# The up projection's steps of 512 columns, two sums on the way out of PSUM, and the first block's convolution moved behind the rest

## The reference

```
h = rms_norm(x, ffn_norm)
u = causal_depthwise_conv(h @ w_up, conv_w, conv_b)     # 256 x 5632
u_gate, u_val = split(u, 2)
x = x + (silu(u_gate) * u_val) @ w_down
```

## Time and profile before

| | us |
|---|---|
| median of three runs | 457.2 |
| the profiled execution | 457.31 |
| its span | 455.0 |
| TensorE busy in the span | 450.9 (99%) |
| VectorE busy | 322.1 (71%) |
| ScalarE busy | 258.2 (57%) |
| GpSimd busy | 55.6 (12%) |
| up stage's channel blocks, from the end of block UP0 to the first down step | 112.88 |
| down stage up to the last step | 60.46 |

### The profile page before, as it was taken

The page is one execution under the profiler, slowest core; times in us unless marked ns, Lnnn a source line. Parts: engine busy times, 40 slices in busy tenths (PEclk is TensorE's granted clock), DMA queues, the critical chain, the costliest instruction groups (busy, mean ns, idle before and its releaser), DMA issues.

```text
span 455.0 us, 7471 instructions
## 1 busy us (share of the span) xinstructions
PE 450.9 (99%) x2965; PEld 412.6 (91%) x2965; DVE 322.1 (71%) x395; ACT 258.2 (57%) x364; POOL 55.6 (12%) x47
## 2 busy tenths in 40 slices
PE   8999999999999999999999999999999999999997
PEld 6889988888888999999999888999999999888886
DVE  4789994876689748772468565898788888884423
ACT  5885453055996668324435366677676767573300
POOL 0100021599350021210000000000000000000000
PEclk9999999999999999999999999999999999999999
DMA  7997657558999326995546354545545544447002
GB/s 260 422 415 253 250 186 230 140 184 213 261 268 310 152 93 208 279 349 183 186 186 270 100 184 187 186 144 223 189 184 184 184 184 184 186 181 281 0 0 94
DMA packets 38154, 92.96 MB, mean 204 GB/s; under 512 B 24816, under 2 KB 25712, under 8 KB 28784
## 3 DMA queue, kind: packets, MB, share of 16 engines
q1 hardware_dynamic: 37712, 91.02, 59.1%
q0 software_dynamic: 416, 1.57, 0.9%
HBM read 85.77 MB, written 1.05 MB: 191 GB/s over the span
## 4 chain that ended last, share of the span: by engine, by line
PE 92%; DMA 4%; DVE 2%; SPq 1%; issue 1%; ACT 1%
PE bank L533 16%; PE bank L534 16%; PE bank L535 16%; PE bank L485 6%; PE bank L487 6%; PE bank L486 6%; PE bank L767 4%; PE bank L764 4%; PE bank L765 4%; DMA w_raw<-weights_dram 4%; PE bank L672 2%; PE bank L670 2%; PE bank L671 2%; PE bank L615 1%; PE bank L628 1%; DVE area L1094 1%
## 5 line engine op out<-in xcount | busy, mean ns | idle before, releaser
L1067 DVE TENSOR_TENSOR w_pair<-w_raw,w_pair 128x2048 fp32r<-128x2048 f32 x73 | 168.1, 2316 | 52.5 <-ACT w_pair L784 52.2
L784 ACT ACTIVATE w_pair<-w_raw 128x2048 fp32r<-128x2048 f32 x73 | 138.5, 1920 | 37.1 <-PE bank L767 17.1
L533 PE MATMUL bank<-h_hi,w_pair 128*128 128x256 f32 x448 | 125.7, 281 | 0.0
L534 PE MATMUL bank<-h_lo,w_pair 128*128 128x256 f32 x448 | 125.1, 279 | 0.0
L535 PE MATMUL bank<-h_hi,w_pair 128*128 128x256 f32 x448 | 125.1, 279 | 0.0
L533 PEld LDWEIGHTS bank<-h_hi,w_pair 128*128 128x128 f32 x448 | 84.2, 188 | 0.1
L534 PEld LDWEIGHTS bank<-h_lo,w_pair 128*128 128x128 f32 x448 | 84.2, 188 | 0.1
L535 PEld LDWEIGHTS bank<-h_hi,w_pair 128*128 128x128 f32 x448 | 84.2, 188 | 0.0
L533 PE MATMUL bank<-a_hi,w_pair 128*128 128x256 f32 x192 | 53.9, 281 | 0.3 <-DVE w_pair L1067 0.3
L534 PE MATMUL bank<-a_lo,w_pair 128*128 128x256 f32 x192 | 53.6, 279 | 0.0
L535 PE MATMUL bank<-a_hi,w_pair 128*128 128x256 f32 x192 | 53.6, 279 | 0.0
(11 more groups left out here) (156 smaller groups left out, 624.3 us busy)
## 6 DMA issues: line engine op xcount, KB each, us to landing
w_raw<-weights_dram SPq DMA_DIRECT2D x73, 1024.0 KB, 5.4
w_raw<-weights_dram SPq DMA_DIRECT2D x8, 256.0 KB, 5.2
w_raw<-weights_dram SPq DMA_DIRECT2D x4, 512.0 KB, 9.0
ys<-x_dram SPq DMA_DIRECT2D x2, 512.0 KB, 8.9
xs<-x_dram POOLq DMA_DIRECT2D x1, 1024.0 KB, 5.5
area<-decay_dram SPq DMA_DIRECT2D x1, 768.0 KB, 8.7
out_dram<-ys SPq DMA_DIRECT2D x3, 256.0 KB, 2.0
xs<-x_chan_dram SPq DMA_DIRECT2D x1, 512.0 KB, 7.1
```

The costliest lines, as they stand in the source:

```text
L533: mm(o, s_hi, r_hi[:, k, :], start=(k == 0 and m % 2 == 0), stop=False)
L534: mm(o, s_hi, r_lo[:, k, :], start=False, stop=False)
L784: A(w_parts(n, r)[0], raw[r][:, :], ACT.Copy).then_inc(hi_ready, 1)
L1067: tt(lo, raw[r][:, :], hi.bitcast(f32), ALU.subtract).then_inc(lo_ready, 1)
```

## The change

Three things change together.

1. `h_hi` and `h_lo` become one tensor `h_pair` [128, 2, 8, 256], and the eight PSUM banks one tensor `banks`. In an up block each output tile has a bank of its own: the stationary high words of the weights meet high and low words of h in one step of 2 x 256 = 512 columns, whose results land in the bank's two halves; the low words of the weights meet h's high words in a step of 256 into the first half. A block takes four banks (0 to 3 or 4 to 7).
2. On the way out the two halves of a bank are added: ScalarE copies the second halves to `u_in` (two copies of 128x512), VectorE adds the first halves to them (`up_sum`, two operations of 128x512), and ScalarE's scaling reads `u_in`. The product `prod` goes from VectorE to GpSimd (`up_prod`). The order within a round changes: on ScalarE reads, split, SiLU, split, high word; on VectorE sums, low word of the block before, filter, split, split.
3. The first block (UP0) is no longer turned by TensorE: GpSimd sorts its 16-bit words into planes (`up_planes`), two transposing DMAs in SP's queue turn them (`up_was_turned`, behind the loads of halves 51 and 52), and its join, scaling, filter, SiLU, product and words come in the down stage, behind the splits of halves 69 to 71. Its two tiles of `a` become the last ones, so the first down half moves to the end of the weights.

```diff
-        h_hi = sb("h_hi", [P, KT, SEQ], f32r)
-        h_lo = sb("h_lo", [P, KT, SEQ], f32r)
+        h_pair = sb("h_pair", [P, 2, KT, SEQ], f32r)
+        h_hi, h_lo = h_pair[:, 0], h_pair[:, 1]
...
-        bank = [ctx.enter_context(nc.psum_tensor(f"bank{i}", [P, 512], f32)) for i in range(8)]
+        banks = ctx.enter_context(nc.psum_tensor("banks", [P, 8, 512], f32))
+        bank = [banks[:, i] for i in range(8)]
...
+            load_rounds((LAST_TURN + 1) // SLOTS - 1, UP_LOADS // SLOTS - 1)
+            for n in range(UP_LOADS, UP_LOADS + 2 * SLOTS):
+                sp.wait_ge(lo_ready, n - SLOTS + 1)
+                sp.dma_start(raw[n % SLOTS][:, :], weights[n]).then_inc(raw_loaded[n % SLOTS], 16)
+                if n in (UP_LOADS + 3, UP_LOADS + 4):
+                    turn_up(n - UP_LOADS - 3)
...
+            def up_prod(jj, silu, values):
+                pool.wait_ge(silu_done, silu)
+                pool.wait_ge(conv_values_done, values)
+                nc.gpsimd.tensor_tensor(prod[:, jj, :, :], conv[:, jj, 0:2, :], conv[:, jj, 2:4, :], ALU.mult)\
+                    .then_inc(prod_ready, 1)
...
-                channel_half([bank[2 * jj], bank[2 * jj + 1]], n, slot, h_hi, h_lo, h).then_inc(half_used, 1)
-
-            up_transposes(0)
+                hi, lo = (w.rearrange("p (k c) -> p k c", k=4) for w in w_parts(n, slot))
+                for m in range(4):
+                    o = bank[4 * jj + m]
+                    for kk in range(4):
+                        k = 4 * h + kk
+                        s_hi, s_lo = hi[:, kk, P * m:P * m + P], lo[:, kk, P * m:P * m + P]
+                        mm(o.rearrange("p (w s) -> p w s", w=2), s_hi, h_pair[:, :, k, :], start=(k == 0), stop=False)
+                        ins = mm(o[:, 0:SEQ], s_lo, h_hi[:, k, :], start=False, stop=(k == KT - 1))
+                ins.then_inc(half_used, 1)
...
+            pe.wait_ge(bank_read[1], UP0 + UP_BLOCKS - 1)
...
                 for j in range(2):
                     A(u_in[:, jj, 2 * j:2 * j + 2, PAD:PAD + SEQ],
-                      bank[2 * jj + j][:, :].rearrange("p (m s) -> p m s", m=2), ACT.Copy)
...
+                      banks[:, 4 * jj + 2 * j:4 * jj + 2 * j + 2, SEQ:2 * SEQ], ACT.Copy).then_inc(up_low_copied, 1)
+                for j in range(2):
+                    act.wait_ge(bank_read[jj], summed + j)
+                    for m in (2 * j, 2 * j + 1):
+                        ins = A(conv[:, jj, m, :], u_in[:, jj, m, PAD:PAD + SEQ], ACT.Identity,
                                 scale=conv_col(4 * m + 2), bias=conv_col(4 * m + 3))
...
             b = UP_BLOCKS - 1
-            up_read(0, DOWN_FIRST_HALF, b - 1, b + 1,
+            up_read(0, DOWN_FIRST_HALF, b - 1, UP0 + b + 1,
                     lambda c: col[:, COL_CONV + 16 * b + c:COL_CONV + 16 * b + c + 1])
-            up_high(0, slice(2 * b, 2 * b + 2), b + 1)
+            up_silu(0, b)
+            up_high(0, slice(2 * b - 2, 2 * b), b)
             for n in range(DOWN_FIRST_HALF + 2, HALVES):
                 split(n)
+                if n == DOWN_FIRST_HALF + 4:
+                    up_first_read()
+                if n == DOWN_FIRST_HALF + 5:
+                    up_high(1, slice(2 * b, 2 * b + 2), b + 1)
...
+            def up_sum(jj, copied):
+
+                for j in range(2):
+                    dve.wait_ge(up_low_copied, copied(j))
+                    part = u_in[:, jj, 2 * j:2 * j + 2, PAD:PAD + SEQ]
+                    tt(part, banks[:, 4 * jj + 2 * j:4 * jj + 2 * j + 2, 0:SEQ], part, ALU.add)                        .then_inc(bank_read[jj], 1)
...
             with dve.Fori(1, UP_BLOCKS // 2) as i:
                 for jj in range(2):
...
+                    up_sum(jj, lambda j: i * 4 + (2 * jj - 2 + j + 1))
+                    up_low(1 - jj, bass.ds(i * 4 + (2 * jj - 4), 2), i * 2 + (jj - 1))
+                    up_conv(jj, lambda j: i * 4 + (2 * jj - 2 + j + 1),
                             lambda c: col[:, bass.ds(i * 32 + (COL_CONV + 16 * jj + c), 1)],
...
                     r = 2 * jj
                     split(i * 4 + (2 * UP0 + 4 + r), r)
-                    up_low(jj, bass.ds(i * 4 + 2 * jj, 2), i * 2 + (jj + 1))
                     r = 2 * jj + 1
                     split(i * 4 + (2 * UP0 + 4 + r), r)
...
+            split(DOWN_FIRST_HALF + 2)
+            up_low(0, slice(2 * b - 2, 2 * b), b)
+            for n in range(DOWN_FIRST_HALF + 3, HALVES):
                 split(n)
+                if n == DOWN_FIRST_HALF + 3:
+                    join_up()
...
+    down = np.concatenate([down[1:], down[:1]])
```

More of the change, by code:

```diff
@@ L147, in hybrid_layer @@
         ret_turned = [area[:, 2048 + 1024 * t:3072 + 1024 * t].bitcast(u16) for t in range(NT)]
+        up_planes = [y_tok[:, t, 512:1024].bitcast(u16) for t in range(NT)]
+        up_turned = [area[:, 7168 + 512 * t:7680 + 512 * t].bitcast(u16) for t in range(NT)]
         PAIR = 2 * 3 * P
@@ L364, in _, with load_rounds, turn_up @@
                     turn_pairs(1 - (LAST_TURN - n) // 2)
[L365 to L368, removed]
+            def load_rounds(first, end):
+                with sp.Fori(first, end) as i:
+                    for r in range(SLOTS):
+                        sp.wait_ge(lo_ready, i * SLOTS + (r + 1))
+                        sp.dma_start(raw[r][:, :], weights[i * SLOTS + (r + SLOTS)]).then_inc(raw_loaded[r], 16)
+            def turn_up(t):
+                sp.wait_ge(up_planes_ready, t + 1)
+                sp.dma_start(up_turned[t].rearrange("p (b s) -> p b s", s=P), up_planes[t], transpose=True)\
+                    .then_inc(up_was_turned[t], 16)
+            UP_LOADS = 2 * UP0 + 4
+            load_rounds((LAST_TURN + 1) // SLOTS - 1, UP_LOADS // SLOTS - 1)
[4 more added lines that the diff above has]
+                    turn_up(n - UP_LOADS - 3)
+            load_rounds(UP_LOADS // SLOTS + 1, ROUNDS)
             for n in range(SLOTS * (ROUNDS + 1), HALVES):
@@ L981, in _, with up_read @@
             up_tok_read(1)
-            def up_read(jj, used, conv_before, read, conv_col):
+            def up_read(jj, used, conv_before, summed, conv_col):
                 act.wait_ge(half_used, used)
@@ L1004, in up_high, with up_first_read @@
                 A(a_hi[:, k, :], prod[:, jj, :, :], ACT.Copy).then_inc(a_hi_ready, 1)
[L1006 to L1015, removed]
+            def up_first_read():
+                act.wait_ge(prod_ready, UP_BLOCKS - 1)
                 act.wait_ge(up_in_ready, NT)
@@ L1027, in _ @@
-            up_high(0, slice(0, 2), 1)
-            up_read(1, 2 * UP0 + 4, None, 2, lambda c: col[:, COL_CONV + 16 + c:COL_CONV + 16 + c + 1])
+            split(2 * UP0 + 4)
+            split(2 * UP0 + 5)
+            up_read(1, 2 * UP0 + 4, None, UP0 + 1, lambda c: col[:, COL_CONV + 16 + c:COL_CONV + 16 + c + 1])
             split(2 * UP0 + 6)
-            up_high(1, slice(2, 4), 2)
+            up_silu(1, 1)
             split(2 * UP0 + 7)
+            up_high(1, slice(0, 2), 1)
             with act.Fori(1, UP_BLOCKS // 2) as i:
@@ L1430, in _, with join_up @@
             steps0 = done[0]
-            order = {0: 1, 2: 2, 3: 3}
+            order = {0: 1, 2: 2}
             split(2 * UP0 + 4)
             split(2 * UP0 + 5)
[L1434 to L1440, removed]
+            def join_up():
+                dve.wait_ge(prod_ready, UP_BLOCKS - 1)
+                for t in range(NT):
+                    dve.wait_ge(up_was_turned[t], 16)
+                    nc.vector.tensor_copy(
+                        u_in[:, 1, :, PAD + P * t:PAD + P * t + P].bitcast(u16).rearrange("p m (s w) -> p w m s", w=2),
+                        up_turned[t].rearrange("p (w m s) -> p w m s", w=2, m=4)).then_inc(up_in_ready, 1)
+            up_sum(1, lambda j: j + 1)
+            up_conv(1, lambda j: j + 1, lambda c: col[:, COL_CONV + 16 + c:COL_CONV + 16 + c + 1],
+                    lambda s: steps0 + order[s])
+            split(2 * UP0 + 6)
             split(2 * UP0 + 7)
```

77 lines of the change are left out of this document (43 added, 34 removed).

## The result

The changed kernel takes 459.27 us (median of 8 runs, 458.01 to 460.75) against 457.23 of the kernel before (8 runs, 456.84 to 459.04): a ratio of 1.0040, 95% interval 1.0026 to 1.0055. It is slower, by about 2 us. The forecast was 455.4 us, and the time lies above its range. The median stands for two kinds of execution: in five of the eight the mean granted clock of TensorE over the span is 0.993 to 0.996 and the time 459.15 to 460.75, in three it is 1.000 and the time 458.01 to 458.30; the profiled execution, 459.39 us, is one of the five.

What follows compares the result with a forecast made beforehand. The prediction took TensorE, busy in 99% of the span at 2.4 GHz, as the bound. Transposes -0.88, steps -2.13 and the wait for half 68 +1.14 made -1.87 us, giving 455.4 us; own range 454.0 to 456.5, overall 453.8 to 459.0.

Steps and rivals of the forecast that it cites:

- VectorE's round: Up stage: sums, low word, filter, two splits and 1.05 us hold-up make 10.93 us, just fitting TensorE's block; cost 0.
- P: Up stage: TensorE's time for one block after the change, 10.99 us.
- second rival: Up stage: VectorE's round overtakes TensorE's, with a product of 1.6 us the excess counts nine times; 458.5 us, chance 14%.
- hold-up: Up rounds: GpSimd's product waits for one split, then delays VectorE's second split by about 1.05 us.
- The steps: TensorE's up stage: removed transposes save 0.88 us and 512-column steps 2.13, together -3.01 us if nothing else comes late.
- Transposes: Up stage: the two groups of four transposes on TensorE go, -0.88 us.
- 512-column step: Up stage: takes 0.2267 us, making a group 0.3433 instead of 0.3500; 320 groups save 2.13 us.
- bounds of 0 and 3.2: Up stage: range in us for the 512-column steps' saving, with a step at 0.2333 or 0.2233 us.
- +1.14 of predicted wait: End of up stage: the last block's chain shifts by 1.54 us against 0.40 to spare; TensorE waits for half 68.
- The product: Moved to GpSimd: 1.25 us alone, far bounds 0.4 and 3.1; in the last chain 0.4 to 2.3.
- third rival: Up rounds: the product gets no turn between two splits, a round becomes 12.5 us; about 469 us, chance 8%.
- What was moved: First block's filter, word copies, transfers and tail, moved within the up stage or to the down stage: gain 0, cost 0.

Runs made afterwards that it cites:

- e5: On top of e1, the input's high and low words laid side by side per tile, so a 512-column step reads one piece: 454.60 us.
- e6: On top of e1, the input's words moved by 32 bytes in SBUF and everything behind them by 64: 461.62 us.
- e2: Changed kernel with the product back on VectorE, between the two splits of a round: 455.16 us, ratio 0.9964 to the kernel before.
- e11: Changed kernel with only half the product on GpSimd, the second tile left out: 455.49 us, ratio 0.9966 to the kernel before.
- e10: Changed kernel with 6 extra unused TensorE steps of 512 columns ahead of half 68: 457.83 us, ratio 1.0015 to the kernel before.
- e9: The changed kernel once more, unedited, on the same chip as e10 and e11: 459.19 us, ratio 1.0043 to the kernel before.
- e8: On top of e1, the first block's join, filter, product and low word in the down stage left out: 454.57 us.
- e1: Changed kernel with halves 68 and 69 split ahead of and inside the last block's chain: 454.42 us, ratio 0.9949 to the kernel before.

## Why the prediction was wrong

The step of the forecast that failed: "VectorE's round becomes 9.88 + 1.05 = 10.93 us against P = 10.99. It just fits [...] Cost 0". The round is 11.32 and the block 11.09, because each round holds a wait for ScalarE that the forecast left out. What follows is the second rival's course, with its place at the last block's chain, and it had been given 14%. Its cause is another, though: it asked for a longer product, but with a block of 11.09 the hold-up alone would have had to pass 11.09 - 9.88 = 1.21 us, and it is 1.13. And that its price, 458.5, comes near is luck: its wait of 2.7 + 1.49 = 4.19 us was 3.21, its steps save 1.07 us too much, and it has no fall of the clock. Term by term:

- **The steps.** Transposes -0.88: right. The 512-column step: 0.2283 and 0.1183 instead of 0.2267 and 0.1167, so -1.07 and not -2.13; inside the bounds of 0 and 3.2. The value was carried over from a step with other operands, and the 256-column step had been taken to keep its length beside it. e5 rules out the two pieces; e6 shows that the place of the operands can make such differences, but what made 0.3433 into 0.3467 stays open.
- **VectorE's round.** Predicted 10.93, measured 11.32. In the round from 381.10 the sums take 1.19 (predicted 1.22), the filter 3.65 (3.65), the splits with the hold-up 5.53 (5.45), the low word until the filter 0.90 (0.61), 11.27 together; here 0.29 is a wait for ScalarE's scaling (0.22 in the row above) and the hand-over behind it. The round before it, from 369.73, has gaps of 0.31 and 0.15 there and takes 11.37. The forecast summed durations and left out that in each round VectorE waits for ScalarE's answer to its own sums: that wait was priced for the last chain and not for the loop. Without it the round would be 11.27 - 0.29 = 10.98 and fit; this is worked out from the trace, and no run took the wait away. e2 and e11 made the round fit by the other term, the hold-up.
- **The lever.** 0.22 us is little in any single round. Over eight it is 1.78 us, and it comes out at half 68: the last sum at 2.72 us behind the block's end instead of 0.83, so +1.14 of predicted wait becomes 3.21 (the chain itself is 0.18 longer).
- **The clock.** Not in the forecast, which had a wait of 1.14 us; by e10 a wait of that size would not have cost it. Behind the wait that the changed kernel has, 3.04 us in the profile, it fell in nine of 13 executions: 1.4 us by the medians of e9 and e10, 1.7 in the profile. Without the fall the kernel takes 458.06, within the forecast's range and still slower than the kernel before.
- **The product.** Alone 1.32 (predicted 1.25, with an upper bound of 2.3 in the last chain that no row gives), hold-up 5.53 - 4.40 = 1.13 (1.05), and it gets its turn between two splits every time: right, and the third rival is out. e2 and e11 agree with the exclusion that the prediction cited from the Trainium skill (SBUF — State Buffer, section Who interferes with whom): with no GpSimd product the split behind it takes 2.29 us, with half a one 2.83, with a whole one 3.40.
- **What was moved.** Nothing at the stage's start, nothing at the end (e8): right.

From the forecast to the time: 455.4 + 1.07 (step) + 1.89 (rounds) + 0.18 (chain) + 1.7 (clock) - 0.47 (start) = 459.8, the profiled execution's own time being 459.39; the rest lies outside the span (459.39 - 457.6 = 1.8 us around it, 2.3 in the profile of before).

## What to carry to other kernels

When two engines run rounds side by side, compare the rounds to a tenth of a microsecond, with every wait for the other engine's answer in them, and multiply the excess by the number of rounds: ask which consumer stands behind the last one. Where slack is 0.06 us of 11, the forecast is a coin toss and its rival deserves more than 14%. And a transfer or split that the next stage needs should not stand in a queue behind a chain it doesn't depend on: moving it forward (e1) made the same slow rounds free.

## What the runs showed of the hardware

- Moving work from VectorE to GpSimd can cost VectorE more than doing it: the product is 0.6 us on VectorE and held VectorE up by 1.1 us from GpSimd.
- A step's length depends on where its operands lie: the same 512- and 256-column steps took 110.93 us over the stage at one place and 113.06 with the input moved by 32 bytes and the operands behind it by 64, and the whole kernel 454.42 and 461.62.
- Behind an idle of 3.04 us TensorE first ran about 1.3 us at its full clock and only then for some 3 us at 1.2 GHz; behind idles of 0.48, 0.60 and 1.65 us (e2, e11, e10) it kept 2.4 GHz. The fall came in nine of the changed kernel's 13 executions.
